# A hybrid decoder step on one NeuronCore: scores of the decode rows on TensorE, and five buffers for the modulation weights

## What is computed

```python
def gathered_dilated_branch(q, kext, vext, rel_bias, window, dilation, past_len):
    nk = window // dilation + 1
    steps = jnp.arange(nk) * dilation
    idx = kext.shape[1] - T + t - steps[None, :]
    kg, vg = kext[:, idx], vext[:, idx]
    s = jnp.einsum('bthe,btkhe->bthk', q, kg)
    ...
    num = jnp.einsum('bthk,btkhe->bthe', p, vg)
# and of the layer, the modulation that every norm and residual uses:
    mod = (jax.nn.silu(c) @ w_ada + b_ada)[:, None, :]
```

## Time and profile before

| | us |
|---|---|
| median of three runs | 2226.62 (2224.72 to 2228.68) |
| the profiled execution, its own time | 2226.02 |
| its span in the trace | 2224.5 |
| `decode_mixers`, first product to first transfer of the next stage | 896.0 to 954.4 |

### The profile page before, as it was taken

One profiled execution on the slowest core, in us unless ns is written; L12 is line 12 of the kernel. 1 busy time (PEld: TensorE's weight loads), 2 busy tenths in 40 slices (PEclk: granted clock), 3 DMA queues, 4 the chain that ended last, 5 costly groups with the idle time before them and its releaser, 6 DMA issues. The chain is left out here.

```text
span 2224.5 us, 40762 instructions
## 1 busy us (share of the span) xinstructions
PE 1991.1 (90%) x13272; PEld 1593.0 (72%) x13273; DVE 1592.1 (72%) x3130; ACT 1050.0 (47%) x2040; POOL 531.6 (24%) x558
## 2 busy tenths in 40 slices
PE   5999999997898988659999479999899998999976
PEld 3788888886777776348888368788677876778732
DVE  2558888986988777769998558764546675658757
ACT  2312111111778888035454247754446564547623
POOL 1013444440111121214555311101100111000056
PEclk8999999998999999779999689999999999999989
DMA  8686555556646477876778179976567887769968
GB/s 249 232 287 236 204 184 185 205 182 214 195 141 221 149 251 267 284 222 206 269 258 268 51 278 397 348 291 247 196 247 244 309 320 274 268 243 377 398 234 312
DMA packets 221182, 553.18 MB, mean 249 GB/s; under 512 B 28793, under 2 KB 43473, under 8 KB 219928
## 3 DMA queue, kind: packets, MB, share of 16 engines
q1 hardware_dynamic: 174045, 431.85, 55.7%
q0 software_dynamic: 25088, 75.71, 9.5%
q10 hardware_dynamic: 21955, 44.42, 5.8%
HBM read 456.95 MB, written 167.56 MB: 281 GB/s over the span
## 5 line engine op out<-in xcount | busy, mean ns | idle before, releaser
L2520 DVE TENSOR_TENSOR LO<-WIDE,HI 128x2048 fp32r<-128x2048 f32 x128 | 287.0, 2284 | 85.0 <-ACT HI L2442 85.0
L620 DVE SCALAR_TENSOR_TENSOR arena<-arena,tapw 128x512 f32<-128x512 f32 (+3 forms) x435 | 266.3, 689 | 0.0
L2442 ACT CAST HI<-WIDE 128x2048 fp32r<-128x2048 f32 x128 | 238.0, 1908 | 20.9 <-PEq L205 16.2
L425 POOL TENSOR_TENSOR STATS<-STATS,K 128x1 f32<-128x1 f32 x16 | 146.5, 9158 | 303.2 <-ACT H L477 303.2
L2520 DVE TENSOR_TENSOR LO<-W2E,HI 128x2048 fp32r<-128x2048 f32 x64 | 143.8, 2289 | 92.1 <-ACT HI L2442 91.6
L1130 ACT ACTIVATE PR<-SBX,NM 128x256 f32<-128x256 f32 (+1 forms) x384 | 171.8, 456 | 1.9 <-DVE NM L1057 1.8
L752 PE MATMUL PJ<-WIN_H,HTH 128*128 128x512 f32 x640 | 161.6, 395 | 10.0 <-ACT HTH L483 10.0
L762 PE MATMUL PJ<-WIN_L,HTH 128*128 128x512 f32 x640 | 158.7, 390 | 0.0
L756 PE MATMUL PJ<-WIN_H,HTL 128*128 128x512 f32 x640 | 158.1, 389 | 0.0
L752 PEld LDWEIGHTS PJ<-WIN_H,HTH 128*128 128x128 f32 x640 | 119.4, 189 | 38.7 <-ACT HTH L483 13.5
L2442 ACT CAST HI<-W2E 128x2048 fp32r<-128x2048 f32 x64 | 118.8, 1904 | 59.7 <-issue 39.2
(11 more groups left out here) (360 smaller groups left out, 4425.7 us busy)
## 6 DMA issues: line engine op xcount, KB each, us to landing
WIDE<-in_w_expert_gate SPq DMA_DIRECT2D x64, 1024.0 KB, 8.4
WIDE<-in_w_expert_up SPq DMA_DIRECT2D x64, 1024.0 KB
W2E<-in_w_expert_down SPq DMA_DIRECT2D x64, 1024.0 KB
expert_rows<-YE ACTq DMA_DIRECT2D x40, 512.0 KB
expert_rows<-NOROWS POOLq DMA_DIRECT2D x11, 1536.0 KB, 11.7
X<-in_x_prompt SPq DMA_DIRECT2D x31, 512.0 KB, 7.9
WAD<-in_w_ada SPq DMA_DIRECT2D x13, 1024.0 KB, 7.2
QN<-q_rows SPq DMA_DIRECT2D x48, 256.0 KB, 3.4
```

The costliest lines, as they stand in the source:

```text
L425: pool.tensor_tensor(MS[:], SSQ[:], const("eps"), ALU.add).then_inc(ms_ready, 1)
L620: ins = nc.vector.scalar_tensor_tensor(out=out, in0=src, scalar=tap, in1=out, op0=ALU.mult, op1=ALU.add)
L2442: nc.scalar.copy(HI[n][:, cols], raw[n][:, cols]).then_inc(hi_ready[n], 1)
L2520: nc.vector.tensor_tensor(LO[n][:, cols], raw[n][:, cols], HI[n][:, cols], ALU.subtract).then_inc(lo_ready[n], 1)
```

## The change

The cached keys are no longer multiplied with the queries by DVE and POOL. Each piece of keys (one row, one branch: 128 positions x 512 numbers, 24 pieces) is turned on PE by four transposes of 128 x 128 into one of three PSUM buffers, and copied back over the keys in `dec_k`, the even pieces by ACT and the odd ones by DVE. The query rows are turned once (4 small transposes) and spread by two multiplications with a mask (`qmask`) into block-diagonal weights `QZ`. The scores of four rows are then 16 products of 384 columns (`scores`), 4 column groups side by side, which leave all 8 rows in one PSUM buffer `SCP`. The small tiles of the softmax have 128 partitions instead of 64 (half of the rows in each block of 32 are not used). The 2 MB of `dec_q` are not loaded any more. In its place lie two more buffers of the modulation ring, so that ring has five: halves 3 and 4 are loaded in rounds 45 and 46, and SP issues 11 halves instead of 13, each when the half five places before it has been used. The small constants of this stage (`DECODE_CONSTANTS`, 128 x 944) are loaded by ACT in round 12 rather than at the start (the first load of constants has 418 columns instead of 546), and the load of `OWN` is gone. The order of PE and ACT in the stage is new. The diff, cut to its core (the constants' construction, tiles of other widths, names):

```diff
             for name, shape in (("dec_k", [P, DEC, 3, DATT]), ("dec_v", [P, DEC, 3, DATT])):
                 state[name] = both.enter_context(nc.sbuf_tensor(name, shape, F32))
-            state["dec_in"] = [lasting(f"dec_{x}_in") for x in "qkv"]
-
-            state["ada"] = both.enter_context(nc.sbuf_tensor("WAD", [P, ADA_RING, KD // 2, 512], F32))
-            state["ada_in"] = [lasting(f"dec_ada_in{n}") for n in range(ADA_RING)]
+            state["dec_in"] = [lasting(f"dec_{x}_in") for x in "kv"]
+
+            state["wad"] = both.enter_context(nc.sbuf_tensor("WAD", [P, ADA_RING, KD // 2, 512], F32))
+            more = state["arena"][:, 0:2 * KD // 2 * 512].rearrange("p (a k n) -> p a k n", a=2, n=512)
+            state["ada"] = [state["wad"][:, n] for n in range(ADA_RING)] + [more[:, n] for n in range(2)]
+            state["ada_in"] = [lasting(f"dec_ada_in{n}") for n in range(len(state["ada"]))]
+            first, last = const_at[DECODE_CONSTANTS[0]][0], sum(const_at[DECODE_CONSTANTS[-1]])
+            state["dec_const"] = both.enter_context(nc.sbuf_tensor("DECCONST", [P, last - first], F32))
+            state["dec_const_at"], state["dec_const_in"] = slice(first, last), lasting("dec_const_in")
             if stop_after >= 2:
                 prompt_attention(nc, t, scratch, const, state)
...
+                    for x, at in enumerate((33, 35, 14, 45, 46)):
                         if g == at:
-                            if x < 2:
+                            if x > 2:
+                                act.wait_ge(conv_out, 16 * KC)
+                            elif x < 2:
 
                                 act.wait_ge(mx_done, 8 * (x + 1) * 4 * SEGMENT)
                             col, ks = (MOD_FIRST + x // 2) * 512, slice(x % 2 * KD // 2, (x % 2 + 1) * KD // 2)
-                            act.dma_start(state["ada"][:, x], t["w_ada"][0].rearrange("(k p) n -> p k n", p=P)[:, ks, col:col + 512]).then_inc(state["ada_in"][x], 16)
-                    if g == 46:
-                        act.wait_ge(conv_out, 16 * KC)
-                        act.dma_start(state["dec_q"], dr["dec"][0:1].to_broadcast([P, DEC, DATT])).then_inc(dq_in, 16)
...
-        TMP, TMPP, SC = sb("TMP", [P, 3, DATT]), sb("TMPP", [P, 3, DATT]), sb("SC", [P, 3, BH])
-        QK0, S0, S0X, N0 = sb("QK0", [DEC, DATT]), sb("S0D", [DEC, HEADS]), sb("S0X", [DEC, DEC, HEADS]), sb("N0", [BH, 1])
-        SS, PE_, MXD, NMD, LD, RD = sb("SS", [BH, KEYS + 3]), sb("PE_", [BH, KEYS + 3]), sb("MXD", [BH, 1]), sb("NMD", [BH, 1]), sb("LD", [BH, 1]), sb("RD", [BH, 1])
-        P0, P0X, P8 = sb("P0", [BH, 1]), sb("P0X", [BH, HEADS]), sb("P8", [DEC, HEADS])
...
         MIX = sb("MIXD", [DEC, D])
-        OWN = sb("OWN", [P, DATT])
-        own_in = sem("own_in")
...
+        N0P, P8P, AT = SMALL[:, 0:1], SMALL[0:DEC, 8:16], CP
+        QTP = SMALL[:, 32:64].rearrange("p (c b) -> p c b", b=DEC)
+        PTP = PT[:, 0:KEYS].rearrange("p (n k) -> p n k", n=3)
+        TK = [OD[0], OD[1], PT]
+        PIECES = 3 * DEC
         MP = [ps(f"MPD{p}", [P, P]) for p in range(2)]
 
         rows_in, conv_in = sem("rows_in"), sem("conv_in")
...
-
+                    sp.dma_start(WA[x % RINGS], w[:, half * KD // 2:(half + 1) * KD // 2, col:col + 512]).then_inc(ada_in[x % RINGS], 16)
+
+                sp.dma_start(R[:], dr["dec"].rearrange("n b c -> b n c")).then_inc(rows_in, 16)
                 for n in range(2):
                     sp.dma_start(BA[:, n], t["b_ada"][0:1, (MOD_FIRST + n) * 512:(MOD_FIRST + n + 1) * 512]).then_inc(b_in[n], 16)
-                sp.dma_start(R[:], dr["dec"].rearrange("n b c -> b n c")).then_inc(rows_in, 16)
-                for x in range(RINGS, 2 * RINGS):
-                    weights(x)
-                at, width = const_at["ownhead"]
-                sp.dma_start(OWN[:], t["constants"][:, at:at + width]).then_inc(own_in, 16)
-                for x in range(2 * RINGS, 2 * NCH):
+                for x in range(RINGS, 2 * NCH):
...
-                pool.wait_ge(dq_in, 16)
-                pool.wait_ge(dk_in, 48)
-                for n, b in enumerate(BY_POOL):
-                    if n:
-                        pool.wait_ge(odd_red, n)
-                    pool.tensor_tensor(TMPP[:], CK[:, b], QB[:, b, None, :].to_broadcast([P, 3, DATT]), ALU.mult).then_inc(odd_mul, 1)
                 pool.wait_ge(var_ready, 1)
                 pool.tensor_tensor(VE[:], MV[:, 1:2], const("eps", DEC), ALU.add).then_inc(rs_ready, 1)
                 pool.wait_ge(rs_ready, 1)
...
@@ -1411,25 +1413,33 @@
                             col = (MOD_FIRST + n + 2) * 512
                             act.dma_start(BA[:, n % 2], t["b_ada"][0:1, col:col + 512]).then_inc(b_in[n % 2], 16)
 
+                def take_keys(pieces):
+                    for x in pieces:
+                        act.wait_ge(keys_turned, x + 1)
+                        nc.scalar.copy(CK[:, x // 3, x % 3], TK[x % 3][:]).then_inc(even_keys, 1)
+
                 act.dma_start(ST[:], t["state_conv"].rearrange("b (w c) -> (b w) c", w=TS).rearrange("(n r) c -> r n c", n=2)).then_inc(conv_in, 16)
                 for b in range(4):
                     act.dma_start(CWR[b * TS:(b + 1) * TS, :], t["conv_w"][0, 0:TS, :]).then_inc(conv_in, 16)
                 for dst, src in ((WL, t["conv_w"][0, TS:TAPS, :]), (CB, t["conv_b"]), (LG, t["ln_g"]), (LB, t["ln_b"])):
                     act.dma_start(dst[:], src.to_broadcast([DEC, DCONV])).then_inc(conv_in, 16)
-                take_modulation(range(3))
+                take_modulation(range(1))
+                take_keys(range(0, 18, 2))
+                take_modulation(range(1, 2))
                 act.wait_ge(new_psum, 1)
                 nc.scalar.copy(N0[:], N0P).then_inc(new_there, 1)
-                take_modulation(range(3, 6))
+                take_keys(range(18, PIECES, 2))
+                take_modulation(range(2, 4))
                 act.wait_ge(step, 4)
                 nc.scalar.activation(PE_[:], SS[:], ACT.Exp, bias=NMD[:], scale=1.0, accum_out=LD[:]).then_inc(exp_ready, 1)
-                take_modulation(range(6, 7))
                 act.wait_ge(p8_psum, 1)
                 nc.scalar.copy(P8[:], P8P).then_inc(p8_ready, 1)
                 act.wait_ge(cstep, 7)
...
-                    if n:
-                        dve.wait_ge(even_red, n)
-                    nc.vector.tensor_tensor(TMP[:], CK[:, own[n]], QB[:, own[n], None, :].to_broadcast([P, 3, DATT]), ALU.mult).then_inc(even_mul, 1)
-                    dve.wait_ge(even_mul, n + 1)
-                    reduced(own[n], TMP, even_red)
-
-                def pool_scores(n):
-                    dve.wait_ge(odd_mul, n + 1)
-                    reduced(BY_POOL[n], TMPP, odd_red)
-
-                own_scores(0)
-                dve.wait_ge(rows_in, 16)
+                def take_keys(pieces):
+                    for x in pieces:
+                        dve.wait_ge(keys_turned, x + 1)
...
                 nc.vector.tensor_tensor(QK0[:], R[:, 0], R[:, 1], ALU.mult).then_inc(new_step, 1)
-                pool_scores(0)
...
                 nc.vector.tensor_tensor(ST[:], ST[:], CWR[:, None, :].to_broadcast([4 * TS, 2, DCONV]), ALU.mult).then_inc(taps_ready, 1)
-                pool_scores(1)
...
-                own_scores(3)
-                pool_scores(2)
-                own_scores(4)
...
+                def turn_keys(pieces):
+                    for x in pieces:
+                        if x > 2:
+                            before = x - 3
+                            pe.wait_ge(odd_keys if before % 2 else even_keys, before // 2 + 1)
+                        for p in range(KC):
+                            mm = nc.tensor.transpose(TK[x % 3][:, p * P:p * P + P], CK[:, x // 3, x % 3, p * P:p * P + P], const("ident"))
+                        mm.then_inc(keys_turned, 1)
+
+                def scores(g):
+                    pe.wait_ge(even_keys, 6 * g + 6)
+                    pe.wait_ge(odd_keys, 6 * g + 6)
+                    for p in range(KC):
                         for q in range(4):
-                            mm = nc.tensor.matmul(MP[n % 2][q * 32:q * 32 + 32], const("ones", 1)[:, 0:32], BA[:, n % 2, q * P:q * P + P], start=False, stop=True)
-                        mm.then_inc(mod_in_psum, 1)
-
-                modulation(range(3))
+                            mm = nc.tensor.matmul(SCP[q * 32:q * 32 + 32, :], QZ[:, p, g * 4 + q], CK[:, g * 4 + q, :, p * P:p * P + P],
+                                                  start=g == 0 and p == 0, stop=g == 1 and p == KC - 1)
+                    return mm
+
+                modulation(range(2))
+                pe.wait_ge(dk_in, 48)
+                turn_keys(range(6))
+                pe.wait_ge(rows_in, 16)
+                for p in range(KC):
+                    mm = nc.tensor.transpose(QTP[:, p], R[:, 0, p * P:p * P + P], const("ident", DEC)[:, 0:DEC])
+                mm.then_inc(q_turned, 1)
```

(17 more changed lines are left out.)

167 lines of the change are left out of this document (88 added, 79 removed).

## The result

| | us |
|---|---|
| kernel before, 20 runs | 2229.15 median (2220.96 to 2232.4) |
| changed kernel, 20 runs | 2233.61 median (2228.79 to 2238.89) |
| ratio | 1.0024, 95% interval 1.0014 to 1.0033 |
| profiled executions, span, before and after | 2224.5 and 2229.2 |
| the stage, PE's first product to the end of its last bias | 52.60 and 57.22 |

The changed kernel is slower by 0.24%, 5.4 us of 2229.15, with an interval of 3.1 to 7.4; the two medians are 4.5 us apart. The forecast was +5.6. The spans of the two traces differ by 4.7 us.

The account below looks back on a forecast made before the run. The weight stream until near 941, then a tail on PE, bounds the stage; changed, PE's work does. Walk +2.9 and clock +2.7, small terms zero, give +5.6 us: 2226.62 + 5.6 = 2232.2, range 2227.5 to 2239.

Parts of the forecast that it names:

- What bounds the kernel, and what DVE's work is worth: In the stage, weight stream then PE's tail bound; DVE's and POOL's score work has 4.8 us to spare, worth zero.
- The sum of PE's work: Turning keys, scores and queries, less the old turn: 17.6 us more on PE, which idled for 14.3 us.
- The walk: PE's stage step by step at 2.4 GHz: bias 0 as now, to 900.2; last bias ends 951.5, 2.9 us later.
- The softmax's pause: Before the turned probabilities PE idles 2.1 us, as ACT copies chunk 3 before its exponentials, then waits 0.5 for their copy.
- The clock: PE's clock falls near 931, at the softmax; half of `OD` and what precedes it run slow: 2.7 us, bounds 0 to 5.3.
- The last loads: At the stage's end, halves 13 and 14 land at 944.5 and 947.2, half 15 at 949.9; PE waits 1.5 us.
- The small terms: First load 0.2 us gained, ACT's two more attention transfers 0 to 0.8, others; sum set at zero.
- B: Rival: the clock stays at 2.4 GHz through the softmax's pause; +2.9 us, 2229.5; 18%.
- C: Rival: the clock falls while keys are turned, near 904 to 919; +13.7 us, 2240, or halfway +8; 15%.
- D: Rival: not slower, as PE does not wait for half 15 at the stage's end; +1.3 or +0.2 us, 2226.8; 11%.
- E: Rival: faster by over 0.2%, stage ending by 944.1, though PE's work alone ends at 946.6; 6%.
- The row at 548.4: Sign for the clock: from 548.4 to 551.8 PE did only transposes, 2.88 us of 3.4, and the clock stayed at 0.50.

Follow-up runs that it names:

- the second profile: The changed kernel measured and profiled once more, nothing altered: 2233.41 us, ratio 1.0025 against the kernel before, stage 56.40 us.
- the first profile: The profiled execution of the changed kernel from its first measurement (2233.61 us median of 20 runs): span 2229.2 us, stage 57.22 us.
- the order on PE: Changed kernel with bias rows first, exponentials before chunk 3's copy, state transfers early, halves 8 to 10 moved forward on PE: 2223.34 and 2221.31 us.
- the early state transfers: Changed kernel with the two convolution-state transfers issued behind half 6 instead of half 15: 2233.25 us, ratio 1.0035 against the kernel before.

## Why the prediction was right, and where it was not

**What bounds the kernel, and what DVE's work is worth**: right. Without four of DVE's five multiplications the kernel before was not faster (1.0006).

**The sum of PE's work**: right. Pieces follow one another at 0.48 us for a forecast of 0.53 (six from 920.13 to 923.03), 1.1 us less in all; a group of scores takes 2.6 (915.88 to 918.48) for 2.65, `OD` 5.36 for 5.3. The modulation was priced too high: a chunk takes 2.3 us (940.03 to 942.31) and not 2.6, a half alone 1.0 and not 1.1. So PE was to be busy for over 50 us and was for 49.4. The stall of 0.6 us for the masked queries was 0.33 and 0.55. Leaving out half of the turning gave back its time, so PE sets the end, as forecast.

**The walk, its first step**: wrong by 1.4 to 2.1 us. I took chunk 0's bias "as now", to 900.2. The diff has `DROWS` moved ahead of the bias rows on SP's queue, and I had a sentence for each queue but this one. PE waited for a row of 2 KB. With the order of before the wait was gone. This is the largest term that I missed, and it had a sign that one could see in the diff.

**The softmax's pause**: right in place and cause, 1.77 + 0.52 us for a forecast of 2.1 + 0.5. DVE waited 4.8 us for ACT ahead of its division, and PE for DVE, as said, and taking chunk 3 after the exponentials removed it:

```profile
DVE RD L1490 <- ACT PE_ L1434: 4.8, 1, 4.8
```

**The clock**: right in size within the range given for it, but not as one event. I charged 2.7 us for a fall behind the softmax's pause. It came in the second profile, at 1.6 us (6.97 - 5.36). In the first it came behind the wait that I had missed, at 905.3, where two pieces took 1.92 us for 1.09, the next one 1.06 for 0.60 and the queries 0.59 for 0.41, 1.5 us more. In both it fell again at the end, behind the waits for the last halves, which I had not priced: the last half and its bias took 0.9 more in the first (from 953.1), halves 14 and 15 took 1.2 more in the second (1.93 and 1.46 for 1.08). So the fall behind the pause was mis-sized by 1 us and did not come in every run, and the falls at the end made up for it: 2.4 and 2.8 us in all for the 2.7 charged. That the sum fits so well is luck.

**The last loads**: right mechanism, short by 0.9 to 1.6 us. I had PE wait only for half 15, 1.5 us; it waited for 14 and for 15, 1.8 + 1.3 and 1.8 + 0.6. The issues were on time: counted from the stage's start, halves 13 and 15 went out at 43.3 and 47.2 us (941.15 and 945.08), where the walk has 42.9 and 47.2. The step that failed is the landing: the walk has half 14 usable at 51.2 and 15 at 53.9, and they were at 52.4 and 54.9. The 2.7 us from one half to the next held (2.5 from 14 to 15); what was short is the time from the issue of 13 to the use of 14, 9.1 us for 5.6 + 2.7. The 5.6 comes from a half that I called alone in the queue; it was issued at 925.21, and the half ahead of it, issued at 920.51, could be used only at 927.88. Besides, PE was ready for half 14 at 50.6, 0.7 earlier than in the walk. That the issues hang on PE reaching halves 8 to 10 was shown by moving these: the waits fell to 0.3 us.

**The small terms** set at zero: PE's first product of the attention came 0.4 us earlier (545.85 for 546.24), for a forecast of 0.2. The attention lost 2.3 us in the first profile, outside 0 to 0.8, and 0.3 in the second.

**The sum.** The walk has 55.5 us of stage at full clock and 58.2 with the clock's fall, 5.6 more than before. The two profiles have 57.2 and 56.4, 4.6 and 3.8 more, so the stage was forecast 1.0 to 1.8 us too long. In the first profile half 15 was issued at 47.2 us, as in the walk at full clock: up to there the missed wait for the bias row (2.1) and the slow stretch behind it (1.5) stood against pieces, halves and chunks that were shorter than priced. Behind it the late landing cost 1.0 us and the slow last half 0.7. The median of after lay 1.4 us above the forecast, while before was itself 2.5 above the runs that I went by, so by the medians the difference is 4.5 us and by the ratio 5.4 (3.1 to 7.4), for a forecast of 5.6. The mechanism held, an engine with more work than it had idle time; the agreement within 0.2 us is luck.

**The rivals.** B, the clock kept through the softmax's pause, is what the first profile shows there, but with a fall elsewhere. C did not come: the clock was 1.00 in the long turning of both profiles, from 908.7 and from 901.0 on. D, no wait for half 15, did not come either; it took another order on PE to get it. E did not come, but its bound was wrong: it has PE's work alone end at 946.6, 50.6 us after the start, and with the order on PE the stage took 48.1 and 48.5 us, 4.5 and 4.1 us less than before, at the mark of 4.5 that E sets or near it.

## What to carry to other kernels

Where an engine's work grows to fill another's idle time, count what stands in its way at each entry: here 7.8 us of waits beside 49.4 of work decided between slower and faster, and order took all but 1.4 of them. Before moving work to another engine, reorder the old kernel to fill the tail that motivates the move: here that gave 3.6 us without the change, and the change, ordered as well, only 0.5 to 0.9 more in the stage. A ring that is refilled as its reader gets to it needs its last reads early in the reader's program, ahead of long work of another kind; and a small transfer on which an engine waits goes first in its queue.

## What the hardware showed that I had not expected

**Transposes kept the clock, and it rose behind them.** From 905.3 to 908.7 PE did nothing but transposes of 128 x 128 and the four small ones of the queries, at 0.50, and from 908.7 on the clock was 1.00, with little else but turning until 915 (one half of the modulation, 1.08 us). In the second profile the clock was 1.00 from 901.0 to 931.7, through all 24 pieces. By the Trainium skill (TensorE: Matmul & The Clock Gate, Part 4: PE-mode transpose) transposes don't count as PE being busy in the same way and don't engage the full clock; these rows, of fp32 transposes, do not agree; no other form was run here. The row at 548.4, which I took as agreeing, had PE idle for 0.5 of 3.4 us; it says nothing of transposes as such.

**The same pause does not always cost the clock.** With the same 1.8 + 0.5 us ahead of `OD` the clock fell in the second profile, with three buffers, with half of the turning and with the early state transfers (`OD` 6.8 to 7.05 us), and was kept in the first and with the bias rows first (`OD` 5.4). Behind the two waits for the last halves it fell to 0.50 in every version that had them, and never in those that had not.

**Halves issued into an idle queue landed later than the walk has them.** By the earlier trace rows I took 5.6 us for the first and 2.7 for each behind it. Of the last three of the changed kernel, issued at 941.15, 942.03 and 945.08 after the DMA had been idle (share 0.00 from 939 to 942), the second could be used 8.2 and the third 7.7 us after its issue, with PE waiting for both; by 5.6 and 2.7 it would have been 7.4 and 7.1. From the issue of the first to the use of the second were 9.1 to 9.5 us in six of the seven profiles that wait so (8.0 with half of the turning), and the third came 2.5 behind it in all six. The state's two transfers are not the reason, as the run that moved them shows. What is, stays open.
